# Feed-forward blocks of a hybrid decoder trunk: the two output columns of a weight block advance together

## The reference

```
x = x + 0.5 * rmsnorm(swiglu(rmsnorm(x)))      feed-forward, D_FF = 2816
x = x + rmsnorm(mix(rmsnorm(x)))               three token mixers, gated merge, output projection
x = x + 0.5 * rmsnorm(swiglu(rmsnorm(x)))      second feed-forward
swiglu(x) = (silu(x @ wg) * (x @ wu)) @ wd
```

## Time and profile before

| | |
|---|---|
| median of 3 runs | 2038.95 us (2038.08 to 2039.51) |
| span of the profiled execution | 2037.9 us, 36447 instructions |
| TensorE matmul busy | 1990.9 us, 98% |
| TensorE weight load busy | 1779.0 us, 87% |
| VectorE busy | 1304.6 us, 64% |
| ScalarE busy | 779.2 us, 38% |
| mean granted TensorE clock | 0.997 |

### The profile page before, as it was taken

One profiled execution on the slowest core, in us unless ns is written; L12 is line 12 of the kernel. 1 busy time (PEld: TensorE's weight loads), 2 busy tenths in 40 slices (PEclk: granted clock), 3 DMA queues, 4 the chain that ended last, 5 costly groups with the idle time before them and its releaser, 6 DMA issues.

```text
span 2037.9 us, 36447 instructions
## 1 busy us (share of the span) xinstructions
PE 1990.9 (98%) x15192; PEld 1779.0 (87%) x15192; DVE 1304.6 (64%) x1997; ACT 779.2 (38%) x932; POOL 84.5 (4%) x164
## 2 busy tenths in 40 slices
PE   7999999999999999999999999999999999999998
PEld 6999988777677798999999999987776778999998
DVE  5776387666467676655377755866665676676644
ACT  4444363322332344333344444623324223443332
POOL 1111000000000000000011100000000000000000
PEclk9999999999999999999999999999999999999999
DMA  6888533343323343444458874333443334434442
GB/s 242 306 299 281 185 110 111 116 128 124 136 107 118 134 166 104 144 144 165 165 191 309 300 245 154 132 109 116 137 136 116 115 114 149 145 106 150 156 159 95
DMA packets 60844, 327.03 MB, mean 160 GB/s; under 512 B 7249, under 2 KB 7441, under 8 KB 34481
## 3 DMA queue, kind: packets, MB, share of 16 engines
q1 hardware_dynamic: 43200, 262.99, 37.5%
q0 software_dynamic: 17520, 62.27, 8.6%
HBM read 290.87 MB, written 34.36 MB: 160 GB/s over the span
## 4 chain that ended last, share of the span: by engine, by line
PE 92%; DVE 4%; ACT 1%; DVEq 1%; DMA 1%; issue 1%; SPq 0%
PE dps L702 45%; PE dps L606 11%; PE dps L556 10%; PE mx L756 9%; PE dps L641 8%; PE mx L923 1%; PE mx L658 1%; PE dps L629 1%; DMA raw<-in_wstream 1%; PE mx L939 1%; PE mx L976 1%; PE mx L953 1%; DVE tmp L1791 1%; DVE rs L1483 1%; PE mx L556 1%; DVE ho L1425 1%
## 5 line engine op out<-in xcount | busy, mean ns | idle before, releaser
L1053 ACT ACTIVATE whi<-raw 128x2048 fp32r<-128x2048 f32 (+1 forms) x144 | 269.2, 1869 | 487.3 <-PE dps L702 470.3
L702 PE MATMUL dps<-uh,whi 128*128 128x320 f32 x1408 | 430.2, 306 | 19.8 <-DVE wlo L1422 15.1
L1422 DVE TENSOR_TENSOR wlo<-raw,whi 128x2048 fp32r<-128x2048 f32 x136 | 311.7, 2292 | 209.0 <-ACT whi L1053 203.9
L702 PE MATMUL dps<-uh,wlo 128*128 128x320 f32 x1408 | 434.3, 308 | 0.0
L702 PE MATMUL dps<-ul,whi 128*128 128x320 f32 x1408 | 433.0, 307 | 0.0
L702 PEld LDWEIGHTS dps<-uh,whi 128*128 128x128 f32 x1408 | 264.8, 188 | 25.2 <-issue 18.5
L702 PEld LDWEIGHTS dps<-uh,wlo 128*128 128x128 f32 x1408 | 264.9, 188 | 0.0
L702 PEld LDWEIGHTS dps<-ul,whi 128*128 128x128 f32 x1408 | 264.0, 187 | 0.6
L606 PE MATMUL dps<-u,raw 128*128 128x320 f32 x768 | 235.7, 444 | 0.0
L702 PE MATMUL dps<-hfh,whi 128*128 128x320 f32 x704 | 220.4, 313 | 0.0
L702 PE MATMUL dps<-hfh,wlo 128*128 128x320 f32 x704 | 217.6, 309 | 0.0
(11 more groups left out here) (295 smaller groups left out, 3191.0 us busy)
## 6 DMA issues: line engine op xcount, KB each, us to landing
raw<-in_wstream SPq DMA_DIRECT2D x198, 1024.0 KB, 4.8
u<-in_wstream POOLq DMA_DIRECT2D x44, 512.0 KB, 7.0
split_store<-wha POOLq DMA_DIRECT2D x44, 512.0 KB, 7.5
raw<-in_wstream SPq DMA_DIRECT2D x44, 512.0 KB, 4.1
parts<-split_store SPq DMA_DIRECT2D x44, 512.0 KB, 5.2
hs<-in_st_hgrn POOLq DMA_DIRECT2D x8, 512.0 KB, 5.7
out_o_hgrn<-hs POOLq DMA_DIRECT2D x8, 512.0 KB, 2.9
out_yT<-x SPq DMA_DIRECT2D x2, 1280.0 KB, 4.5
```

Of the source, the lines that this page charges most:

```text
L702: m = pe.matmul(dps[:, 2 * half + c, 0:T], w[:, k, c * P:(c + 1) * P], v[:, k0 + k, :], start=first and k == 0 and i == 0, stop=last and k ...
L1053: return nc.scalar.activation(out, in_, f, **kw)
L1422: return nc.vector.tensor_tensor(out, a, b, op)
```

## The change

For all calls of `split_tiles` but the first gate block and the last down block, the loop over the two columns moves from the outside to the inside. For each tile k the order is now: high weights of column 0 and of column 1 with the high activations, high weights of both with the low activations, low weights of both with the high activations. So the bank alternates from matmul to matmul, each moving tile is used by two matmuls in a row, and each of the two weight tensors is read from the two columns in turn, 512 bytes apart. Within a bank the order of the additions stays the same, and so does the place of `block_done`.

```diff
             def split_tiles(s, kt, hi, lo_, half, first=True, last=True, k0=0, norm=None, ends=None):
 
                 wh, wl = (v[s][:, 0:kt * 256].rearrange("p (k n) -> p k n", k=kt) for v in (whi, wlo))
+                if not norm and not ends:
+                    for k in range(kt):
+                        for i, (w, v) in enumerate(((wh, hi), (wh, lo_), (wl, hi))):
+                            for c in range(2):
+                                m = pe.matmul(dps[:, 2 * half + c, 0:T], w[:, k, c * P:(c + 1) * P], v[:, k0 + k, :],
+                                              start=first and k == 0 and i == 0, stop=last and k == kt - 1 and i == 2,
+                                              skip_group_check=True)
+                    m.then_inc(S["block_done"], 1)
+                    return
                 order = [(c, k, 0) for c in range(2) for k in range(kt)]
```

## The result

The changed kernel takes 2041.71 us (median of 20 runs, 2040.74 to 2044.84) and the one before 2038.44 us (median of 20 runs, 2035.38 to 2041.71). The ratio is 1.0019, with a 95% interval of 1.0013 to 1.0025: slower by 3.9 us, between 2.7 and 5.1 (the two medians are 3.3 us apart). The forecast was 2043.4, +0.22%.

The account below looks back on a forecast made before the run. PE was taken to bound the kernel, busy for 98% of the span. Span 2037.9 + 4.5 for gate/up, 0 for bank, repeated tile and down, gave 2042.4; the runs' median lies 1.05 higher, so 2043.4 us, range 2029 to 2049.

Parts of the forecast that it names:

- PE's spacing is what sets the end: Whole kernel: PE holds 92% of the path, so changed matmul spacing goes into the end time one for one.
- (1): Reordered feed-forward matmuls: changing the bank at every matmul costs 0.
- (2): Reordered feed-forward matmuls: using the same moving tile twice in a row costs or saves 0.
- (3): Weight-load order in gate/up: one credit per six matmuls instead of two, +1.1 ns x 4032 = +4.5 us.
- credit: Gate/up: 6.7 ns less per three matmuls, 433.3 against 440 in down, read as earned once per excursion.
- excursion: Weight loads going to another weight tensor and back: once in three matmuls before, once in six after.
- Down: Down stages: no credit to lose, 0, or at best one new credit per six matmuls, -2.2 us.
- The total loss of the credit: Rival in gate/up: the credit needs the short cycle of three, +9.0 us, 2048; chance 0.18.
- No net change: Rival: wlo pair earns two credits per six, or down's gain pays gate/up's loss; 2037 to 2041 us; chance 0.22.
- A cheap repeated tile: Rival: repeated moving tile is cheap in steady state, gate/up -4.5 us, down -6.6, 2028; chance 0.17.
- That PE is limited by the number of its weight loads alone: Rival: loads match matmuls one to one and none is removed, so 2039 us; counted within no net change's 0.22.

Follow-up runs that it names:

- bank_only: Kernel before, same order of weights and activations, output alternating between the two banks at every matmul: gate/up 144.45 ns per matmul, down 146.65.
- low_weights_second: Kernel before, each triple reordered to high weights x high part, low x high, high x low: gate/up 144.46 ns per matmul, down 146.68.
- pairs_in_column: Kernel before, one column after the other, two contraction tiles advancing together, two of each product in a row: gate/up 145.56 ns per matmul, down 146.13.
- ov_plus_64: Kernel before, 64 bytes of padding in front of ov, moving whi, hfh, hfl and ov: gate/up 146.67 ns per matmul, down 146.67.
- wlo_plus_64_new_order: Changed kernel plus padding: wlo moved 64 bytes, whi, hfh, hfl and ov 256: gate/up 146.67 ns per matmul, down 146.6; 2048.07 us.
- wlo_plus_64: Kernel before, old order, wlo moved 64 bytes, whi, hfh, hfl and ov 256: gate/up 144.45 or 146.67 ns per matmul, down 144.5; 2038.83 us.
- triples_alternate: Kernel before, the two columns alternating triple by triple: gate/up 144.45 ns per matmul, down 146.65; 2043.51 us against 2039.87 before on the same chip.
- ov_plus_192: Kernel before, old order, 192 bytes of padding in front of ov: gate/up 145.56 ns per matmul, down 144.48.
- wlo_plus_32: Kernel before, old order, wlo moved 32 bytes, whi, hfh, hfl and ov 256: gate/up 146.66 ns per matmul, down 146.67.

## Why the prediction was right, point by point

**PE's spacing is what sets the end.** Right. The change of the paces gives +3.3 us and the comparison of the runs +3.9 (2.7 to 5.1); no other engine, wait or transfer shows a trace of it.

**(1) The bank costs nothing.** Right, shown by bank_only: 144.45 and 146.65.

**(2) A repeated moving tile costs nothing.** Right, shown by low_weights_second, where one gap in three is of that kind.

**(3) One credit per excursion, so one in six.** Right for gate/up: 145.56 was forecast as 145.6, and pairs_in_column shows that the grouping of the products alone carries the change. Three qualifications. The prediction gave the credit to the weights' excursion; the moving tiles make the same one (uh, ul, uh), and no run separates the two. The count of excursions is a law only where the placement lets an excursion pay (ov_plus_64, wlo_plus_64_new_order). And the prediction's reading, an effect of going to another tensor, was too narrow: ov_plus_64 leaves the tensors as they are and takes the credit away.

**Down.** The term was 0, with -2.2 us as its other end, and it measured -1.1: the new order runs at 146.13 there, on average as if it had one credit in twelve matmuls, and the old one at 146.66. Taking 0 for it was wrong, and why down gains without a short gap stays open. This is nearly the whole difference of the sum: 4.5 forecast, 3.3 from the paces. I had this case in the range and took the wrong end for the point.

**The rivals.** The total loss of the credit (2048) didn't come, but it was near: the same order at the placement of wlo_plus_64_new_order has no credit in gate/up and took 2048.07 us. No net change is excluded by the interval for the ratio, which begins at 1.0013, although the effect, 0.19%, is smaller than the 0.2% that the prediction counted as telling from no change; 20 runs of each kernel resolve it. Its mechanism was there in part: down pays back 1.1 of the 4.4 us that gate/up loses. A cheap repeated tile is excluded by (2). That PE is limited by the number of its weight loads alone is excluded, since order and placement change the pace at an equal number.

**The profile that was to be seen.** The forecast named 146.6 us between the second start of gate/up and the first of down; 146.43 for one gap less is 146.57. Down was to stay at 74.6 and took 74.38.

What stays open is the cause inside the chip: why a credit is 6.7 ns, what an excursion at the right distance avoids, whether it is that of the weights or that of the moving tiles, and what picks one of two paces in wlo_plus_64. No run here looks below the start of a matmul. That the period is 256 bytes is supported (gate/up and down become alike where their distances are alike modulo 256, twice) but no placement that differs by 256 bytes alone was run.

## What to carry to other kernels

Where one engine issues back to back and is on the whole path, read the spacing of starts over a thousand instructions, not busy time or single-run totals: it resolved 0.01 ns per matmul here, while totals scattered by 6 us. When a reordering moves that spacing, split it into its parts (bank, repeated moving tile, alternation between the columns, grouping of the products) before believing any of them; here three of four were nothing. And before tuning the order, try a few paddings in front of the operands: 128 bytes in two places gave 4.7 us, where no order tried gained anything.

## What the runs showed of the hardware

- With fp32r operands of 128 x 128 and 128 x 320, back to back at the full granted clock, the spacing was never below 144.4 nor above 146.7 ns on average over a stage. In between lie a few values, 145.56, 146.11 to 146.13, 146.2, 146.6, that stay the same in all four blocks. The two down stages with a pause stand apart (147.1 in triples_alternate, 145.0 in ov_plus_192). No single gap in these stages was below 139 ns.
- The addresses of the operands alone move the spacing over that whole range (ov_plus_64 and ov_plus_192), and 32 bytes are enough (wlo_plus_32). The Trainium skill (TensorE: Matmul & The Clock Gate, Step-by-step: what each phase is for) says that loading the next weights doesn't steal read bandwidth from the running matmul. No run here measures bandwidth, but the matmuls' spacing isn't indifferent to where the weights lie: in wlo_plus_32 of the operands of split_tiles only the low weights moved, and gate/up went from 144.45 to 146.66. The same page's formula (Back-to-back issue gap), 135.8 ns for 320 columns, is given there for an isolated matmul and not for a stream of weight loads and matmuls; no gap of these stages reached it in any of the 14 profiles.
- The same code at the same addresses ran a stage at 144.45 in two places and at 146.67 in two others of one execution (wlo_plus_64). A pace, once taken, held to the end of the stage.
